# Up projection of a conv-FFN: the high and low parts of x as one 512-column moving operand

## The reference, cut to what matters

```
up = h @ w_up                                  # [256, 2048] @ [2048, 11264]
up_pad = pad(up, two zero rows in front)
conv = conv_b + sum(up_pad[:, j:j + s] * conv_w[j] for j in range(3))
gate, val = split(conv, 2)
return (gelu(gate) * val) @ w_down             # [256, 5632] @ [5632, 2048]
```

## Time and profile before

| | |
|---|---|
| runs | 3488.84 us median of 3 (3486.52 to 3490.53) |
| the profiled execution | 3482.98 us, its span 3481.2 us |
| PE busy | 3193.5 us, 92% of the span |
| DVE busy | 1662.0 us, 48% |
| ACT busy | 1288.3 us, 37% |
| stretch of the up stage | about 1150 to 1660 us of the span |

### The profile page before, as it was taken

One profiled execution on the slowest core, in us unless ns is written; L12 is line 12 of the kernel. 1 busy time (PEld: TensorE's weight loads), 2 busy tenths in 40 slices (PEclk: granted clock), 3 DMA queues, 4 the chain that ended last, 5 costly groups with the idle time before them and its releaser, 6 DMA issues.

```text
span 3481.2 us, 50282 instructions
## 1 busy us (share of the span) xinstructions
PE 3193.5 (92%) x20248; PEld 2759.2 (79%) x20248; DVE 1662.0 (48%) x2591; ACT 1288.3 (37%) x1920; POOL 17.4 (0%) x33
## 2 busy tenths in 40 slices
PE   6988888978986899999999899999998968999997
PEld 6956666646975899999999688778887848889886
DVE  4334444434551655565444522445453366336755
ACT  3321111125433554444443422444442223236542
POOL 0000000000000000000000000000000000000000
PEclk8989999989987999999999999999999989999998
DMA  7545554456531355555555322222223213224442
GB/s 223 183 181 193 193 193 190 169 203 250 184 133 49 126 185 184 181 181 173 167 175 179 130 87 95 85 73 94 85 82 128 97 48 121 91 102 144 138 154 107
DMA packets 73152, 500.97 MB, mean 144 GB/s; under 512 B 8332, under 2 KB 8460, under 8 KB 20176
## 3 DMA queue, kind: packets, MB, share of 16 engines
q1 hardware_dynamic: 69264, 477.69, 39.2%
q0 software_dynamic: 3776, 21.70, 2.0%
HBM read 492.79 MB, written 6.55 MB: 143 GB/s over the span
## 4 chain that ended last, share of the span: by engine, by line
PE 83%; DVE 8%; ACT 4%; DMA 3%; issue 2%; SPq 0%; ACTq 0%; DVEq 0%
PE bank L669 41%; PE bank L998 7%; PE bank L738 5%; PE bank L1029 5%; PE bank L1031 5%; PE bank L1030 5%; DMA ring_f<-in_w_in 3%; PE bank L790 2%; DVE ring_f32r L1564 2%; PE bank L718 1%; ACT high_f32r L1163 1%; DVE x_f L1561 1%; PE bank L601 1%; PE bank L1061 1%; PE bank L973 1%
## 5 line engine op out<-in xcount | busy, mean ns | idle before, releaser
L1564 DVE TENSOR_TENSOR ring_f32r<-ring_f,high_f32r 128x1024 fp32r<-128x1024 f32 (+1 forms) x692 | 780.4, 1160 | 807.0 <-ACT high_f32r L1163 806.0
L669 PE MATMUL bank<-y_f32r,high_f32r 128*128 128x256 f32 (+1 forms) x3168 | 978.4, 309 | 56.6 <-DVE h_f32r L1564 32.4
L1163 ACT CAST high_f32r<-ring_f 128x1024 fp32r<-128x1024 f32 (+1 forms) x692 | 657.0, 999 | 957.3 <-PE bank L669 665.3
L669 PE MATMUL bank<-h_f32r,high_f32r 128*128 128x256 f32 (+1 forms) x2400 | 756.7, 315 | 0.9 <-DVE ring_f32r L1564 0.9
L669 PE MATMUL bank<-y_f32r,ring_f32r 128*128 128x256 f32 (+1 forms) x2464 | 747.7, 303 | 0.0
L669 PEld LDWEIGHTS bank<-y_f32r,high_f32r 128*128 128x128 f32 x3168 | 610.0, 193 | 87.2 <-issue 47.4
L669 PEld LDWEIGHTS bank<-y_f32r,ring_f32r 128*128 128x128 f32 x2464 | 475.7, 193 | 17.0
L669 PEld LDWEIGHTS bank<-h_f32r,high_f32r 128*128 128x128 f32 x2400 | 462.2, 193 | 28.2 <-DVE ring_f32r L1564 1.3
L669 PE MATMUL bank<-z_f32r,high_f32r 128*128 128x256 f32 x912 | 261.2, 286 | 10.3 <-DVE h_f32r L1564 7.4
L738 PE MATMUL bank<-h_f,ring_f 128*128 128x256 f32 x768 | 207.6, 410 | 28.5 <-DMA ring_f<-in_w_in 28.5
L1029 PE MATMUL bank<-h_f32r,high_f32r 128*128 128x512 f32 x512 | 209.4, 409 | 0.0
(11 more groups left out here) (411 smaller groups left out, 4627.4 us busy)
## 6 DMA issues: line engine op xcount, KB each, us to landing
ring_f<-in_w_in SPq DMA_DIRECT2D x159, 1024.0 KB, 4.9
ring_f<-in_w_mod SPq DMA_DIRECT2D x96, 1024.0 KB, 6.9
ring_f<-in_w_up SPq DMA_DIRECT2D x88, 1024.0 KB, 4.9
ring_f<-in_w_out SPq DMA_DIRECT2D x48, 1024.0 KB, 4.9
ring_f<-in_w_down SPq DMA_DIRECT2D x64, 704.0 KB, 4.1
ring_f<-in_w_kv SPq DMA_DIRECT2D x8, 1024.0 KB, 4.8
x_f<-in_ctxT POOLq DMA_DIRECT2D x2, 2048.0 KB, 12.0
ring_f<-in_w_q SPq DMA_DIRECT2D x4, 1024.0 KB, 4.8
```

The costliest lines, as they stand in the source:

```text
L669: last = mm(bk[(t0 + j) % banks][:, 0:width], w[:, c], x[:, k], start=(k == 0 and w is hi and x is rhs.hi), stop=(k == KC - 1 and w is lo))
L1163: act.copy(w_hi[p % 2][:, half], slot[s % SLOTS][:, half]).then_inc(w_high, 1)
L1564: return v.tensor_tensor(out, in0, in1, op)
```

## The change

A `Split` whose high and low parts lie in areas Y0 and Y1 gets, for each chunk, one view over both (`both`), 512 columns in two runs of 256. For `up`, the hi·hi and hi·lo matmuls become one of 512 columns, which leaves hi·hi in columns 0 to 255 of the bank and hi·lo in columns 256 to 511; lo·hi stays as it was. So a tile has 32 matmuls. The halves must then be added: ACT copies the second half to a new buffer `up_sum`, DVE adds the first half to it, and ACT's Identity and DVE's taps read `up_sum` in place of the bank. `gemm_free` is raised by DVE's add; the taps have their own semaphore `f_taps`. The low part of x moves from area H0 to Y1, so parts 1 and 2 of the products' high halves change places, and one wait of ACT behind `down` is for its last matmul instead of its last but one slab.

```diff
+        def pair(one, two):
+            a = arena_r[:, one:one + T]
+            (step, n), (inner, width) = a.ap
+            return bass.AP(a.tensor, a.offset, [[step, n], [(two - one) * inner, 2], [inner, width]])
...
+                if (h_at, l_at) == (Y0_AT, Y1_AT):
+                    self.both = [pair(h_at + k * T, l_at + k * T) for k in range(KC)]
...
-               "up": Split((H0_AT, 1), (Y0_AT, 1), (H0_AT, 1)),
+               "up": Split((H0_AT, 1), (Y0_AT, 1), (Y1_AT, 1)),
...
+        up_sum = [f1.take(T) for _ in range(2)]
...
-        ACT_AT = (H1_AT, Y1_AT, H0_AT)
+        ACT_AT = (H1_AT, H0_AT, Y1_AT)
...
 # TensorE, gemm3
+                        if name == "up":
+                            mm(bk[(t0 + j) % banks][:, :], hi[:, c], rhs.both[k], start=(k == 0), stop=False)
+                            last = mm(bk[(t0 + j) % banks][:, 0:width], lo[:, c], rhs.hi[:, k], start=False, stop=(k == KC - 1))
+                            continue
...
 # ScalarE, up
                 act.wait_ge(gemm_done, i * 4 + (TILE0["up"] + j + 1))
+                act.wait_ge(S("f_taps"), i * 4 + (j + 1))
+                act.copy(up_sum[j % 2], bk[(TILE0["up"] + j) % 4][:, T:]).then_inc(S("f_half"), 1)
+                act.wait_ge(gemm_free, i * 4 + (TILE0["up"] + j + 1))
                 par = at(convf, i * 4 + j)
-                f(cv[j % 4], bk[(TILE0["up"] + j) % 4][:, 0:T], ACT.Identity, scale=par[:, 2:3], bias=par[:, 3:4]
+                f(cv[j % 4], up_sum[j % 2], ACT.Identity, scale=par[:, 2:3], bias=par[:, 3:4]
                   ).then_inc(S("f_part"), 1)
                 high(ahead[0], j + ahead[1], i)
                 if j % 2:
-                    act.wait_ge(gemm_free, i * 4 + (TILE0["up"] + j))
+                    act.wait_ge(S("f_taps"), i * 4 + (j + 2))
...
 # ScalarE, behind down
-                    act.wait_ge(S("down_used"), 3 * 16)
+                    act.wait_ge(gemm_done, TILE0["down"] + 16)
...
 # VectorE, up
-                dve.wait_ge(S("f_part"), i * 4 + (j + 1))
-                par, b, c = at(convf, i * 4 + j), bk[(TILE0["up"] + j) % 4], cv[j % 4]
+                par, bank, c, b = at(convf, i * 4 + j), bk[(TILE0["up"] + j) % 4], cv[j % 4], up_sum[j % 2]
+                dve.wait_ge(S("f_half"), i * 4 + (j + 1))
+                tt(b, bank[:, 0:T], b, ALU.add).then_inc(gemm_free, 1)
+                dve.wait_ge(gemm_free, i * 4 + (TILE0["up"] + j + 1))
+                dve.wait_ge(S("f_part"), i * 4 + (j + 1))
                 stt(c[:, 1:T], b[:, 0:T - 1], par[:, 1:2], c[:, 1:T], op1=ALU.add).then_inc(S("f_tap"), 1)
...
-                stt(c[:, 2:T], b[:, 0:T - 2], par[:, 0:1], c[:, 2:T], op1=ALU.add).then_inc(gemm_free, 1)
+                stt(c[:, 2:T], b[:, 0:T - 2], par[:, 0:1], c[:, 2:T], op1=ALU.add).then_inc(S("f_taps"), 1)
                 low(ahead[0], j + ahead[1], i, (1,))
                 if j % 2:
-                    dve.wait_ge(gemm_free, i * 4 + (TILE0["up"] + j + 1))
+                    dve.wait_ge(S("f_taps"), i * 4 + (j + 3))
...
+            dve.sem_inc(S("f_taps"), 2)
```

More of the change, by code:

```diff
@@ L316, in build @@
                "kv": Split((H1_AT, 1), (Y1_AT, 1), (H1_AT, 1)), "q": Split((H0_AT, 1), (Z28_AT, 1), (H0_AT, 1)),
-               "up": Split((H0_AT, 1), (Y0_AT, 1), (H0_AT, 1)), "in20": Split((H0_AT, 2), (Y0_AT, 2), (X0_AT, 2)),
+               "up": Split((H0_AT, 1), (Y0_AT, 1), (Y1_AT, 1)), "in20": Split((H0_AT, 2), (Y0_AT, 2), (X0_AT, 2)),
                "in20_late": Split((H0_AT, 2), (H0_AT, 2), (X0_AT, 2)), "out20": Split((Y0_AT, 2), (H0_AT, 2), (Y0_AT, 2)), "in21": Split((H0_AT, 1), (Y0_AT, 1), (H0_AT, 1)),
```

## The result

| | before | after |
|---|---|---|
| first comparison, median of 5 runs each | 3490.53 us (3486.52 to 3492.37) | 3509.36 us (3505.70 to 3511.74) |
| the same kernels again, 23 and 12 runs | 3490.07 us | 3501.10 us (3497.30 to 3509.14) |

The first ratio is 1.0049 with a 95% interval of 1.003 to 1.0068, or +17 us (+10.5 to +23.7). The second is 1.0037 (1.0022 to 1.0052), or +13 us (+7.7 to +18). One of the 23 runs of before took 6468.67 us and is left out of the ratio. The change makes the kernel slower by some 0.4%. Forecast were +5 us and 3494 us, with a range that ended at 3509: the first median lies 0.4 us above it, the second within it. Counted as differences from the 3488.84 us on which the forecast stands, the range is -9 to +20 us, and both +17 and +13 lie within it.

The account below looks back on a forecast made before the run. PE was taken to bound the up stage. Terms of -19.1, +17.2, +4.1 and +3.2 summed to +5.4 us, giving 3494 us from 3488.84, with a range of 3480 to 3509.

Parts of the forecast that it names:

- What bounds it: Up stage: PE sets the pace; the next tile's preparation by ACT and DVE has 0.83 us of slack.
- Term 1: Tiles 0 to 85 at PE's pace: wide matmuls save 0.222 us a tile, -19.1 us.
- Term 2: Stalls of PE in 41 ordinary tile pairs, 0.34 us each or 0.54 with the product gate: +17.2 us.
- Term 3: Around `act_lows(0)`, tiles 61 to 63: copy, add and queueing lengthen the chain that ACT and DVE set, +4.1 us.
- Term 4: From tile 85 into down, where the chain of waits is off PE: +3.2 us.
- Handoffs are dear: Rival: each pass between ACT and DVE in the up stage costs 0.16 us, not 0.03; +21 us, 3510; chance 0.18.
- The wide matmul saves less: Rival: in the up stage a tile saves only 0.04 us of PE's time; +13 us, 3502; chance 0.05.
- The chain fits: Rival: up-stage register work is hidden, -4 us, 3485, or the chain fits wholly, -12, 3477; chance 0.14.
- The clock falls: Rival: brief PE pauses in each pair put a tenth of the up stage at 1.2 GHz, +45 us; chance 0.03.
- At nothing: Costed at zero: two other taps, bank release, weights' DMA, exchange of areas, and ACT's moved wait behind down.

Follow-up runs that it names:

- e3b: The changed kernel with only chunk 0 of a tile wide, the 15 others as two narrow matmuls into the two bank halves; 3512.3 us, ratio 1.0049.
- e5: The changed kernel with ACT's casts ahead of the Identity and DVE's `low` ahead of the taps; 3482.47 us, ratio 0.9977.
- e2: The changed kernel's matmuls with the evacuation of before, the bank's second half read by nobody; 3473.67 us, ratio 0.9962.
- e6: The changed kernel with scale and bias of Identity and taps taken from a fixed address that needs no register; one run, 3498.73 us.
- e10: The changed kernel unaltered, measured and profiled a second time; 3501.1 us, ratio 1.0037.

## Why the prediction was off, step by step

**What bounds it: right.** PE had the pace and ACT and DVE the slack, and the slack of 0.83 us was the thing to watch. e3b and e5 show it from both sides: the chain alone costs 14 us in the stage (some 1.6 of them the clock's), and all of its work costs 0.6 us once the casts no longer stand behind it.

**Term 1, the gain at PE's pace: mis-sized, and this is the step that failed.** The prediction said "I take 226 for a wide one between narrow ones too", from a stage in which all matmuls are wide. A chunk then costs 345.9 ns and a tile saves 0.222 us. Measured are 353 ns in most tiles, a saving of 0.106 (e2), and 347 in the others, 0.21. At 353, the term is 86 x 0.106 = -9.1 us instead of -19.1. With the 28 tiles at 347 it is some 3 us more; how much of that PE keeps, and does not spend waiting for the chain, no run measured. By the formula that the Trainium skill gives for the distance of a single matmul ("TensorE: Matmul & The Clock Gate", "Back-to-back issue gap"), one instruction less would save an estimated 2.5 ns a chunk. The runs show 6.6 and 13.

**Term 2, the pairs: the chain right, the sum too high for the same reason.** The chain is 5.83 us where 5.87 was forecast, copy, add, handoffs and register work each within 0.03. But a slower PE also leaves less to stall: 5.83 - 5.65 = 0.18 an ordinary pair instead of 0.34. The product gate's extra was sized 0.2 and is 0.3, since from the one-element Gelu to the copy it is 0.39 us, not 0.3. 20 x 0.18 + 18 x 0.48 = 12.2 instead of 17.2. Check against the ledger: 30 pairs of 5.65 + 5.83 and 14 gates of 0.3 give 348.6; measured 348.4.

**Term 3, `act_lows(0)`: right, but for the clock.** Forecast +3.4 for what ACT and DVE set there, with 0.7 on top of it for PE's being early; 61 to 65 shows +3.1. In the second profile it is +4.7, since the granted clock fell to 0.50 behind the pause, which the term had not counted.

**Term 4, into down: right.** +3.2 forecast, 26.55 - 23.37 = +3.2 measured, twice.

Put together with the measured sizes: -9.1 + 12.2 + 3.7 + 3.2 = +10.0, where the profiles show +10.9 and +11.7, the second with 1.6 of the clock's in it. Of the 5.5 to 6.3 us that the forecast was short, 4.6 come from these two sizes.

**The rivals.** *Handoffs are dear* gave 3510, closest to the first median, and is refuted: the handoffs are 0.03 to 0.04 us, the chain was not longer than forecast. That its number fits is accident. *The wide matmul saves less* was the mechanism, less strongly than it was priced: a tile saves 0.106 us, where that rival had 0.04 and the forecast 0.222 (+10 rather than +13). *The chain fits*: that the register work is hidden is refuted by e6, and that the chain fits wholly by the stalls of after. *The clock falls*, because of the brief stall of each pair, is refuted: the granted clock of the stage is 1.00 in both profiles of after, over more than 60 stalls. It does fall once in the second, for 3.4 us behind the 3.2 us pause in front of tile 65, and costs 1.6 us where the rival had +45. The Trainium skill (same page, "A second HAM failure mode: psum-queue depth-cycling") tells of a clock that swings as PE idles briefly between groups of matmuls. The trace agrees for none of the short stalls, and shows one fall behind the long one.

**At nothing:** bank release, the exchange of areas and the moved wait did cost nothing (behind down 1809.2 and 1809.6). What the page of one profile can't give is the first loop. It made +13.4 us of the first profile's difference and +3.2 of the second's. The change has no code there, and fourteen profiles scatter by 17 us in it: the 0.2% that was called "no change" is less than half of that. Of the first comparison's +17 us some 6 are not accounted for by the stage. In e10 the difference is +13 and the interval holds the stage's +11.7; whether the 6 were scatter is not shown beyond that.

## What to carry to other kernels

A change that takes work from the bounding engine and lengthens the chain behind it is judged by the chain's slack for one unit, not by the busy time of its engines, and slack is spent first by what is written ahead of the work that the bound engine waits for: put the copies, sums and activations behind the casts, and the same change turns from +11 us to -7 in the stage and its end (-8 in the medians). Take an instruction's distance from a place with the same neighbours, or bound it from both sides; a saving of 14 ns times 1376 is 19 us, and half of it was not there. In a loop, count the register work in front of an instruction as part of the chain if it stands behind the wait.

## What the runs showed of the hardware that was not expected

PE has two paces for the same alternation of a 512-column and a 256-column float32r matmul at the same granted clock: 353 and 347 ns for the two. It keeps one through a whole tile, in the five kernels without stalls in the loops through all 87, and in after changes it at 20 boundaries between tiles, each with a stall; sixteen wide ones in a row, then sixteen narrow ones, cost 348 for the two. What selects the pace is open.

Pauses of equal length can end with or without a fall of the granted clock: behind 3.1 to 3.3 us in front of tile 65 it fell to 0.50 for 3.4 us in four profiles and stayed at 1.00 in the fifth, with the same kernel as one of the four.

Address work in registers costs ACT 0.20 us behind a wait (1.07 against 0.87 us from copy to Identity), though the address does not depend on what is waited for. The pass of a tile between ACT and DVE, where it holds no such work, costs 0.03 to 0.04 us.
